# All sums of the seven-product down stage on VectorE, the next tile pair's ahead of this one's low part, and the residual work later in the pair

## What is computed

```python
u, val = jnp.split(h2 @ p['w_up'], [D_FF], axis=-1)          # D_FF = 2816
u, fbuf_new = causal_dwconv(u, fbuf, p['ffconv_w'], p['ffconv_b'])
x = x + g2 * ((jax.nn.silu(u) * val) @ p['w_down'])          # w_down: 2816 x 1024
...
y_prompt = rms_norm(h_p, final_w).astype(x_prompt.dtype)
```

## Time and profile before

| | us |
|---|---|
| median of 3 runs (lowest, highest) | 2769.14 (2765.73, 2771.17) |
| profiled execution | 2766.77 |
| its span | 2765.0 |
| busy in the span: PE, DVE, ACT, POOL | 2467.0, 1877.4, 910.1, 602.1 |
| down stage, first pair (2256.4 to 2366.7) | 110.3 |
| down stage, other seven pairs (2366.7 to 2742.6) | 375.9 |
| from there to the end of the span | 22.4 |

### The profile page before, as it was taken

The page is one execution under the profiler, slowest core; times in us unless marked ns, Lnnn a source line. Parts: engine busy times, 40 slices in busy tenths (PEclk is TensorE's granted clock), DMA queues, the critical chain, the costliest instruction groups (busy, mean ns, idle before and its releaser), DMA issues. The chain is left out here.

```text
span 2765.0 us, 44410 instructions
## 1 busy us (share of the span) xinstructions
PE 2467.0 (89%) x17028; PEld 1515.4 (55%) x17028; DVE 1877.4 (68%) x3669; ACT 910.1 (33%) x1371; POOL 602.1 (22%) x605
## 2 busy tenths in 40 slices
PE   3699999879989998699889999999999965899997
PEld 0355555568677776455456666666666632344443
DVE  6455555446878877488867777777777768666566
ACT  2324343214444444144422222322222224222222
POOL 0123232300000000022421222212222149323221
PEclk9999999979999999699989999999999988999999
DMA  8335434360242313233322122221222233323323
GB/s 255 104 118 167 148 132 121 124 216 21 84 175 89 120 57 96 64 124 115 110 70 74 49 77 71 77 73 54 71 71 77 70 112 99 102 85 102 100 84 91
DMA packets 197176, 279.87 MB, mean 101 GB/s; under 512 B 18840, under 2 KB 134088, under 8 KB 194876
## 3 DMA queue, kind: packets, MB, share of 16 engines
q1 hardware_dynamic: 197061, 278.35, 31.4%
HBM read 203.02 MB, written 75.29 MB: 101 GB/s over the span
## 5 line engine op out<-in xcount | busy, mean ns | idle before, releaser
L2514 PE MATMUL py<-h_parts,w_heads 128*128 128x384 f16 (+1 forms) x792 | 246.0, 311 | 19.7 <-DVE u_p L2671 19.7
L2515 PE MATMUL py<-h_parts,w_heads 128*128 128x384 f16 (+1 forms) x792 | 245.8, 310 | 0.0
L2516 PE MATMUL py<-h_parts,w_heads 128*128 128x384 f16 (+1 forms) x792 | 245.8, 310 | 0.0
L345 PE MATMUL prj<-w_heads,h_parts_t 128*128 128x512 f16 x512 | 196.2, 383 | 10.8 <-DVE h_parts_t L962 5.4
L345 PE MATMUL d_pm<-d_w,w_heads 128*128 128x512 f16 x392 | 153.5, 392 | 56.4 <-DVE w_heads L2377 56.2
L2377 DVE SCALAR_TENSOR_TENSOR w_heads<-d_a,mscale,w_heads 128x896 f16<-128x896 f32 x87 | 107.7, 1238 | 136.1 <-ACT w_heads L2372 136.1
L346 PE MATMUL prj<-w_heads,h_parts_t 128*128 128x512 f16 x512 | 195.9, 383 | 0.0
L347 PE MATMUL prj<-w_heads,h_parts_t 128*128 128x512 f16 x512 | 195.6, 382 | 0.0
L2840 POOL TENSOR_TENSOR u_vz<-u_val,u_cv 128x384 f32<-128x384 f32 (+1 forms) x66 | 60.2, 912 | 620.0 <-DVE u_cv L2711 406.4
L2372 ACT ACTIVATE w_heads<-d_a,mscale 128x896 f16<-128x896 f32 x87 | 90.6, 1042 | 313.4 <-DVE d_a L2359 221.1
L345 PE MATMUL m_prj<-m_h,w_heads 128*128 128x128 f16 (+1 forms) x1088 | 179.6, 218 | 11.6 <-DMA m_h<-h_parts 10.3
(11 more groups left out here) (535 smaller groups left out, 6189.2 us busy)
## 6 DMA issues: line engine op xcount, KB each, us to landing
C_new<-in_w_up_dram SPq DMA_DIRECT2D x11, 2048.0 KB, 7.6
w_heads<-in_w_up_dram SPq DMA_DIRECT2D x44, 512.0 KB
d_a<-act_cols SPq DMA_DIRECT2D x174, 128.0 KB, 2.2
act_cols<-w_heads SPq DMA_DIRECT2D x44, 384.0 KB, 2.3
win_raw<-in_w_in_dram SPq DMA_DIRECT2D x8, 2048.0 KB, 14.1
win_raw<-in_w_ada_dram SPq DMA_DIRECT2D x8, 2048.0 KB
first_a<-in_w_down_dram SPq DMA_DIRECT2D x22, 512.0 KB, 3.9
wa<-in_w_ada_dram SPq DMA_DIRECT2D x4, 2048.0 KB, 17.6
```

The lines of the kernel that those rows point to most:

```text
L345: nc.tensor.matmul(out, left[0], right[0], start=(k == 0), stop=False)
L2514: nc.tensor.matmul(out, left[0], right[0], start=(start and k == 0), stop=False, skip_group_check=True)
L2515: nc.tensor.matmul(out, left[0], right[1], start=False, stop=False, skip_group_check=True)
L2516: last = nc.tensor.matmul(out, left[1], right[0], start=False, stop=(k == KC // 2 - 1), skip_group_check=True)
```

## The change

`sums_w` is issued to VectorE instead of GpSimd; `sums_13` and `sums_24` become one function `sums_a` with all four activation sums on VectorE. In the first pair VectorE's list is now low part (raw) of block j, weight sums of block j + 1, low part (sums) of j, activation sums of step j + 1, low part of the activations of step j. In later pairs the activation sums of step n + 1 stand ahead of the low part of step n. For block 0 the sums move into group 1 of the up stage's last block. `blocks` loses its two additions from SBUF, which become `late_blocks` one step later, and the scaling, residual, mean and norm of both tiles stand up to one step later (steps 1, 2, 3 and 4, 5, 6 instead of 1, 1, 2 and 3, 4, 5), ScalarE's squares and SyncE's saves and loads likewise. GpSimd keeps the roots and one small sum for the sample tokens. Waits and arithmetic are otherwise as they were.

```diff
-    def sums_w(self, pool, j):
+    def sums_w(self, dve, j):
...
-        self.nc.gpsimd.tensor_tensor(t[:, 2], b22, b12, ALU.subtract)
-        steps.then(self.nc.gpsimd.tensor_tensor(t[:, 0], b12, b11, ALU.subtract))
-        steps.then(self.nc.gpsimd.tensor_tensor(t[:, 1], b22, t[:, 0], ALU.subtract))
-        self.nc.gpsimd.tensor_tensor(t[:, 3], t[:, 1], b21, ALU.subtract).then_inc(self.w_summed, 1)
+        self.nc.vector.tensor_tensor(t[:, 2], b22, b12, ALU.subtract)
+        steps.then(self.nc.vector.tensor_tensor(t[:, 0], b12, b11, ALU.subtract))
+        steps.then(self.nc.vector.tensor_tensor(t[:, 1], b22, t[:, 0], ALU.subtract))
+        self.nc.vector.tensor_tensor(t[:, 3], t[:, 1], b21, ALU.subtract).then_inc(self.w_summed, 1)
...
-    def sums_13(self, pool, n):
+    def sums_a(self, dve, n):
...
-        self.nc.gpsimd.tensor_tensor(a[:, 4], a[:, 0], a[:, 1], ALU.add)
-        self.nc.gpsimd.tensor_tensor(a[:, 6], a[:, 2], a[:, 0], ALU.subtract).then_inc(self.a_half, 1)
-
-    def sums_24(self, dve, n):
-
-        a = self.a_raw(n)
+        self.nc.vector.tensor_tensor(a[:, 4], a[:, 0], a[:, 1], ALU.add)
+        self.nc.vector.tensor_tensor(a[:, 6], a[:, 2], a[:, 0], ALU.subtract).then_inc(self.a_half, 1)
...
-                    if g == 1 and not last:
-                        up.cut_lo_own(dve, b + 1, 1 - u)
+                    if g == 1:
+                        if last:
+                            dn.sums_w(dve, 0)
+                            dn.sums_a(dve, 0)
+                        else:
+                            up.cut_lo_own(dve, b + 1, 1 - u)
                     if g == 2:
                         if last:
-                            dn.sums_24(dve, 0)
                             dn.lo_part(dve, 0, 0)
...
-                if j == 5:
+                if j == 6:
                     save(y_rows[2 * i - 2], 2 * i - 2)
                     load_x(2 * i - 1)
-                if j == 8:
+                if j == 9:
                     save(y_rows[2 * i - 1], 2 * i - 1)
                     load_x(2 * i)
...
-                if j == 2:
+                if j == 3:
                     square(2 * i - 2)
-                if j == 5:
+                if j == 6:
                     square(2 * i - 1)
...
+            dn.sums_w(dve, 1)
+            dn.sums_a(dve, 1)
             for j in range(1, J):
                 dn.lo_part(dve, j, 0)
+                if j + 1 < J:
+                    dn.sums_w(dve, j + 1)
                 dn.lo_part(dve, j, 1)
-                prepare(j)
+                dn.sums_a(dve, j + 1)
+                dn.cut_a_lo(dve, j)
...
             for n in range(J, N):
                 i, j = divmod(n, J)
-                prepare(n)
-                if n == J:
-                    dve.wait_ge(s["const"], 32)
+                if n + 1 < N:
+                    dn.sums_a(dve, n + 1)
+                dn.cut_a_lo(dve, n)
                 if j == 0:
                     blocks(i - 1)
+                if n == J + 1:
+                    dve.wait_ge(s["const"], 32)
                 if j == 1:
+                    late_blocks(i - 1)
                     scale(2 * i - 2)
+                if j == 2:
                     residual(2 * i - 2)
-                if j == 2:
+                if j == 3:
                     mean(2 * i - 2)
                     norm(2 * i - 2)
-                if j == 3:
+                if j == 4:
                     scale(2 * i - 1)
-                if j == 4:
+                if j == 5:
                     residual(2 * i - 1)
-                if j == 5:
+                if j == 6:
                     mean(2 * i - 1)
                     norm(2 * i - 1)
...
-            for j in range(1, J):
-                dn.sums_w(pool, j)
-                dn.sums_13(pool, j)
-            for n in range(J, N):
-                i, j = divmod(n, J)
-                dn.sums_13(pool, n)
-                if j == 3:
-                    x_rms(2 * i - 2)
-                if j == 6:
-                    x_rms(2 * i - 1)
+            for k in range(NCH - 2):
+                x_rms(k)
```

More of the change, by code:

```diff
@@ L2295, in sums_w @@
         p = self.last_user(self.SUM, j)
-        self.w_landed(pool, j)
+        self.w_landed(dve, j)
         if p is not None:
-            pool.wait_ge(self.w_lo, 2 * p + 2)
-        steps = Steps(pool, self.w_steps, 2 * j)
-        self.nc.gpsimd.tensor_tensor(t[:, 2], b22, b12, ALU.subtract)
-        steps.then(self.nc.gpsimd.tensor_tensor(t[:, 0], b12, b11, ALU.subtract))
-        steps.then(self.nc.gpsimd.tensor_tensor(t[:, 1], b22, t[:, 0], ALU.subtract))
-        self.nc.gpsimd.tensor_tensor(t[:, 3], t[:, 1], b21, ALU.subtract).then_inc(self.w_summed, 1)
+            dve.wait_ge(self.w_lo, 2 * p + 2)
+        steps = Steps(dve, self.w_steps, 2 * j)
+        self.nc.vector.tensor_tensor(t[:, 2], b22, b12, ALU.subtract)
+        steps.then(self.nc.vector.tensor_tensor(t[:, 0], b12, b11, ALU.subtract))
+        steps.then(self.nc.vector.tensor_tensor(t[:, 1], b22, t[:, 0], ALU.subtract))
+        self.nc.vector.tensor_tensor(t[:, 3], t[:, 1], b21, ALU.subtract).then_inc(self.w_summed, 1)
     def w_parts(self, j, i):
@@ L2344, in load_a @@
             sp.dma_start(raw[:, c], src[c]).then_inc(sem, 16)
-    def sums_13(self, pool, n):
+    def sums_a(self, dve, n):
         a = self.a_raw(n)
-        pool.wait_ge(self.a_in[3 if n == 0 else n % 3], 32 if n == 0 else 32 * ((n + 2) // 3))
-        self.nc.gpsimd.tensor_tensor(a[:, 4], a[:, 0], a[:, 1], ALU.add)
-        self.nc.gpsimd.tensor_tensor(a[:, 6], a[:, 2], a[:, 0], ALU.subtract).then_inc(self.a_half, 1)
-    def sums_24(self, dve, n):
-        a = self.a_raw(n)
+        dve.wait_ge(self.a_in[3 if n == 0 else n % 3], 32 if n == 0 else 32 * ((n + 2) // 3))
+        self.nc.vector.tensor_tensor(a[:, 4], a[:, 0], a[:, 1], ALU.add)
+        self.nc.vector.tensor_tensor(a[:, 6], a[:, 2], a[:, 0], ALU.subtract).then_inc(self.a_half, 1)
         dve.wait_ge(self.a_half, n + 1)
@@ L2849, in body @@
                     odd_vz(UG * b + g, g, first and g == 0)
-                    if last and g == 0:
-                        dn.sums_w(pool, 0)
-                        dn.sums_13(pool, 0)
             body(0, 0, True)
@@ L3037, in _ @@
             steps = Steps(dve, s["steps"])
-            def prepare(n):
-                dn.sums_24(dve, n)
-                dn.cut_a_lo(dve, n)
             def blocks(i):
@@ L3058, in blocks, with late_blocks @@
                 nc.vector.tensor_tensor(c12, pm[:, 2], c12, ALU.add).then_inc(s["folded"], 1)
+            def late_blocks(i):
                 dve.wait_ge(s["kept"], 2 * i + 2)
-                dve.wait_ge(s["folded"], at + 5)
+                dve.wait_ge(s["folded"], 5 * i + 5)
                 steps.then(nc.vector.tensor_tensor(c22, c22, s5, ALU.add))
@@ L3124, in _ @@
             blocks(PAIRS - 1)
+            late_blocks(PAIRS - 1)
             for k in (NCH - 2, NCH - 1):
```

## The result

The changed kernel takes 2727.28 us (median of 4 runs, 2726.30 to 2729.11) against 2768.62 us of the kernel before in the same runs: a ratio of 0.9852, 95% interval 0.9835 to 0.9869. The gain is 41.3 us where 32.2 were forecast, and the time lies 0.7 us under the lower end of the range. The direction and the mechanism were right; two of the three terms of the sum were too small.

What follows compares the result with a forecast made beforehand. GpSimd was taken to pace the first pair, with late low parts stalling TensorE later; gains 12.0 + 0.8 + 19.4 = 32.2 us led to 2734.6 profiled, 2736.9 by the median, forecast 2737 us, range 2728 to 2747.

Steps and rivals of the forecast that it cites:

- the three terms of the sum: Gains forecast: 12.0 us in the first pair, 0.8 at the up stage's end, 19.4 in the later pairs.
- the three rivals: Stall kept at pair starts (chance 0.11), VectorE staying slow (0.05), weight loads setting the pace (0.06).
- the second rival: First pair: VectorE stays slow and becomes a worse bound, 29 us lost, 20 gained later, 2778 us; chance 0.05.
- the step of 9.2 us: First pair: VectorE's weight step, 1.8 + 2.8 + 2.3 + 1.2 + 1.1 us of low parts and sums.
- The scalars: First pair: ten scalar instructions on VectorE at 0.15 us and their gaps, about 2 us.
- The 0.9 us for a TensorE still at work on step 9: First pair's end: a step 9 of some 7.3 us at low clock would hold step 10 up by 0.9 us.
- the tie at S + 13.6: Later pair start: low part ready 13.55 us after the previous pair's last TensorE step begins (S), wanted at 13.6.
- the allowance of 3 us: Later pairs: 2 us of remaining loss and some 1 us of ordinary step boundaries, of 22.4 us lost.
- The first rival: Later pair starts keep part of their stall, 1.5 us each, giving back 10 us: 2747 us; chance 0.11.
- The cover: Up stage's last block: block 0's sums (4.0 us) are free inside VectorE's 5.47 us idle behind a TensorE transposition.
- the transfers keep their distance: Residual stream's saves and loads move one step with their norm, so what stands behind them keeps its distance.
- The third rival: First pair: weight loads set the pace, 1.4 us late in nine steps, so nothing gained there: 2749 us; chance 0.06.

Runs made afterwards that it cites:

- e9_pool_busy: Changed kernel with 30 dependent multiplications of a private 128x504 tile on GpSimd in the first pair, touching none of the kernel's tiles: 2748.36 us.
- e1_late: Kernel before with only the residual work moved later as in the change, all sums where they were: 2755.30 us.
- e7_pool_a: Changed kernel with the four activation sums of steps 1 to 11 back on GpSimd: 2724.21 us.
- e4_no_late: Changed kernel with folding, scaling, residual, mean, norm, squares, saves and loads back at their old steps: 2735.59 us.
- e5_const: Changed kernel with residual work at its old steps, but the wait for the residual stage's constants one step later, behind the first folding: 2732.65 us.
- e2_ahead: Kernel before with only the later pairs' activation sums all on VectorE, one step ahead: 2749.94 us.
- e3_first_pair: Block 0 and first pair as in the changed kernel, later pairs as in the kernel before: 2752.26 us.

## Why the prediction was right and where it was not

**The bound and the mechanism.** Right. VectorE sets the first pair's pace without idle time, its low parts return to 1.81 and 2.34 us, and GpSimd's silence is the cause (`e9_pool_busy`). In the later pairs it is not silence alone: `e1_late` gains 12.5 us with GpSimd at work. The new time is within 10 us of the forecast with each of the three rivals excluded. The rule of the Trainium skill (Perfetto Trace Analysis, section Optimizing Scalar/DVE Operations) that work may go off a saturated VectorE, which was weighed as the ground of the second rival, holds here for the small sums only: 3 us for the activation sums (`e7_pool_a`).

**The first pair: 12.0 forecast, 16.7 measured.** The term that failed is the step of 9.2 us. It was a sum of rounded durations and of dependent distances; VectorE's cost is the distance from start to start, and half of the sums are not dependent: 8.77. Over the eight steps 2 to 9 that is 3.4 us. The first and the tenth step bring 0.7 and 0.2, of which 0.3 are not this term: block 2 came 7.9 us into the stage, forecast 8.2. The scalars took 2.15 us, the prediction 2. The 0.9 us for a TensorE still at work on step 9, for which the forecast had gone from 12.7 to 12.0, were 0.2. The sum: 12.7 + 4.4 - 0.15 - 0.2 = 16.7.

**The later pairs: 19.4 forecast, 22.3 measured.** The step that failed is the tie at S + 13.6, on which the allowance of 3 us rested. The low part was ready at S + 12.9. The first low part ended 0.2 us sooner than set down, the five foldings took 3.4 us instead of 3.6, and two sets of sums 1.06 instead of 1.2 each. With 0.7 us to spare nothing is lost, in any pair. No run tests these 0.7 us; the 1.1 us of the step before are borne out by `e4_no_late`, where 1.65 us more cost 0.63 in each pair. The first rival (1.5 us lost in each) did not occur.

**The up stage: 0.8 forecast, 0.6 measured.** The cover held. VectorE's idle time ahead of the same copy, 5.47 us in the earlier trace rows, is 1.45 now:

```profile
2230.03 0.17 DVE L2738 COPY u_in_s<-pt 128x16 f32<-128x16 f32 x1 [1.45 <-PE pt L2516]
...
2238.23 2.06 DVE L2322 SCALAR_TENSOR_TENSOR w_heads<-w_heads,mscale 128x1536 f16<-128x1536 f32 x1
```

Of the 0.84 us of the two sums that stood there, 0.25 went back: the low part behind them begins sooner, meets GpSimd's product of 2237.67 to 2238.68 and takes 2.06 us instead of 1.81. From the copy to the down stage it is 25.97 or 25.98 us in three executions with the old order and 25.37 to 25.39 in eleven with the new, so this small term is well measured.

**What the sum left out.** The wait for the constants. The prediction said that the transfers keep their distance, and did not see that VectorE would come to this wait earlier. It cost nothing only because the change moves it too; left where it was it would have taken some 3 us (`e5_const`). The 0.4 us ahead of the copy are no effect of the change: that point lies between 2230.03 and 2235.28 in these executions, of whatever kernel. The 0.4 us after the last matmul (22.3 us also in `e2_ahead` and `e4_no_late`, 22.6 and 22.8 in `e1_late` and `e3_first_pair`) go with the activation sums of the later pairs on VectorE; why was not followed up.

**The range.** It failed by its bounds, not by a rival. The first pair's upper bound was 15 and the later pairs' 21, where its own count of what was lost there, 22.4 us, was excluded by no row. The allowances for losses were taken off the bounds as well as off the forecast.

**Loads.** The third rival did not occur: VectorE waits for a weight load once, in step 1, as forecast, and not in steps 2 to 9. The ground given against it was misread: the kernel before waits for a second block, since GpSimd's first sum of block 10, at 2346.71, stands behind 0.99 us of idle time for the same kind of load.

## What to carry to other kernels

Cost an engine's in-order list by the distance from one start to the next, and look at which instructions depend on their neighbour: over the first pair the 0.4 us a step between that and the durations were nearly 4 us. When the order in front of a wait changes, look at how long before it the transfer was asked for, and read the landing time of the transfer rather than the name in the bracket. Where VectorE and GpSimd are both busy for most of a stage, moving GpSimd's large elementwise work onto VectorE can make the stage faster, since the stretch that GpSimd puts on VectorE's instructions can be longer than the work moved.

## What the runs showed of the hardware that was not expected

GpSimd's slowing of VectorE needs no common data: a private tile does it, with 0.7 to 0.85 us for nearly every VectorE instruction on SBUF while 128x504 multiplications run, and the step goes from 8.77 to 16.6 us. It is a price for each instruction and not a share of the VectorE instruction's length, and it follows the size of GpSimd's instruction: 0.14 to 0.25 us beside sums of 128x128 (`e7_pool_a`). VectorE was back at full speed as soon as GpSimd stopped.

TensorE's clock fell in the middle of a step that had begun at full speed (2343.41, after 4.06 us of idle time), where before the change step 9 began at the lower level after 5.31 us. In the profile of `e4_no_late` an idle time of 2.13 us in a stretch that was otherwise busy was followed by the same fall, and those of 0.47 us were not. The idle time alone does not tell, though: in the kernel before, 2.17 us at the same place (ahead of the matmul of 2378.15) were followed by no fall, and in `e3_first_pair` the same 4.06 us ahead of step 9 had it begin at the lower level (2341.89, 0.61 us). What decides between them was not found.
